# Silu in place of sigmoid and product, new engine orders, and a quarter of the threshold updates on GpSimd

## The reference

```
h = rmsnorm(x) * (1 + scale) + shift                 # adaLN from c
xr, gr, q, k, v, ga, qi, ki, wi = split(h @ w_in)    # 2760 columns
xr = causal conv of width 4;  y_r = rg_lru(xr) * silu(gr)
   gate_x, gate_a = sigmoid(...);  a = exp(-8 gate_a softplus(-a_param))
   h_t = a h_(t-1) + sqrt(1 - a^2) gate_x xr
score = sum over 8 heads of relu(qi . ki) * wi       # causal
idx = top 256 of each row of score                   # blocks of 128 rows
y_a = attention(q, k, v over idx only) * silu(ga)    # 8 heads of 64
x = x + gate * (concat(y_r, y_a) @ w_out);  out = rmsnorm(x)
```

## Time and profile before

| | |
|---|---|
| median of 3 runs (range) | 636.92 us (636.62 to 640.52) |
| the profiled execution | 639.16 us, of which the span is 637.4 us |
| PE busy | 540.3 us, 85% |
| VectorE busy | 444.1 us, 70% |
| ScalarE busy | 374.0 us, 59% |
| GpSimd busy | 247.5 us, 39% |

### The profile page before, as it was taken

One profiled execution on the slowest core, in us unless ns is written; L12 is line 12 of the kernel. 1 busy time (PEld: TensorE's weight loads), 2 busy tenths in 40 slices (PEclk: granted clock), 3 DMA queues, 4 the chain that ended last, 5 costly groups with the idle time before them and its releaser, 6 DMA issues. The chain is left out here.

```text
span 637.4 us, 8051 instructions
## 1 busy us (share of the span) xinstructions
PE 540.3 (85%) x2676; PEld 447.9 (70%) x2676; DVE 444.1 (70%) x996; ACT 374.0 (59%) x678; POOL 247.5 (39%) x207
## 2 busy tenths in 40 slices
PE   2369989979999996999999406478999999999994
PEld 2356868768777773888777305467888999988873
DVE  5985467767998978945778988856456665665532
ACT  7423236544698989865789334464556675656631
POOL 5050853252525466277656400750223030304322
PEclk9859989999999999899999855559999999999999
DMA  8966460341021121035450420030010001011011
GB/s 344 411 204 230 103 152 11 99 100 32 2 66 34 34 64 35 2 99 133 117 148 2 171 93 0 0 99 2 1 67 34 33 2 67 23 45 67 0 67 66
DMA packets 16457, 51.96 MB, mean 82 GB/s; under 512 B 4000, under 2 KB 5024, under 8 KB 15392
## 3 DMA queue, kind: packets, MB, share of 16 engines
q1 hardware_dynamic: 16416, 51.45, 25.6%
HBM read 37.81 MB, written 4.19 MB: 66 GB/s over the span
## 5 line engine op out<-in xcount | busy, mean ns | idle before, releaser
L1384 PE MATMUL pair<-h_hi,w_hi 128*128 128x512 f32 (+1 forms) x352 | 115.7, 411 | 7.7 <-DVE rnn_gr L1187 4.8
L1384 PE MATMUL pair<-h_lo,w_hi 128*128 128x512 f32 (+1 forms) x352 | 111.1, 397 | 0.0
L1384 PE MATMUL pair<-h_hi,w_lo 128*128 128x512 f32 (+1 forms) x352 | 110.1, 394 | 0.0
L1309 DVE TENSOR_TENSOR pt_lo<-pair,pt_hi 128x512 fp32r<-128x512 f32 (+3 forms) x96 | 50.5, 553 | 70.6 <-ACT pt_hi L968 70.2
L863 ACT ACTIVATE bias_sb<-score_sb,tinies 128x1024 bf16<-128x1024 f32 (+2 forms) x93 | 95.7, 1033 | 2.5 <-DVE tinies L1114 2.3
L1384 PEld LDWEIGHTS pair<-h_hi,w_hi 128*128 128x128 f32 (+1 forms) x352 | 65.7, 191 | 25.9 <-issue 13.8
L692 POOL TENSOR_SCALAR w_hi<-w_raw 128x1024 fp32r<-128x1024 f32 (+1 forms) x22 | 26.9, 1223 | 137.8 <-PE pair L1384 122.1
L1384 PEld LDWEIGHTS pair<-h_lo,w_hi 128*128 128x128 f32 (+1 forms) x352 | 66.8, 190 | 16.0 <-issue 1.1
L1384 PEld LDWEIGHTS pair<-h_hi,w_lo 128*128 128x128 f32 (+1 forms) x352 | 66.6, 189 | 15.7 <-issue 0.8
L1100 DVE TENSOR_SCALAR_CACHE_REDUCE bias_sb<-score_sb,tinies 128x640 bf16<-128x640 f32 (+2 forms) x93 | 72.5, 801 | 0.9
L782 POOL TENSOR_TENSOR x_res<-q_free,x_res 128x512 f32<-128x512 f32 x14 | 18.2, 1297 | 120.3 <-DVE q_free L1280 120.3
(11 more groups left out here) (199 smaller groups left out, 1258.9 us busy)
## 6 DMA issues: line engine op xcount, KB each, us to landing
w_raw<-in_w_tiles SPq DMA_DIRECT2D x21, 512.0 KB, 3.6
ada<-in_ada_w SPq DMA_DIRECT2D x8, 1024.0 KB, 18.1
x_sb<-in_x SPq DMA_DIRECT2D x8, 512.0 KB, 6.7
ada_g<-in_ada_w SPq DMA_DIRECT2D x8, 512.0 KB, 4.5
qs<-half_hi SPq DMA_DIRECT2D x16, 256.0 KB, 3.6
qs<-half_lo SPq DMA_DIRECT2D x16, 256.0 KB, 4.4
wo_raw<-in_w_out SPq DMA_DIRECT2D x8, 512.0 KB, 6.7
x_res<-in_x SPq DMA_DIRECT2D x8, 512.0 KB, 3.4
```

Source lines behind the costliest of these rows:

```text
L1309: nc.vector.tensor_tensor(pt_lo[:, 4 * b:4 * b + nc4, hh, :], psum[use % 2][:, 0:nc4 * P].rearrange("p (c q) -> p c q", q=P), f32(pt_hi[:, ...
L1384: ins = nc.tensor.matmul(psum[banks[half]][0:width, :], w[b][:, k, 0:width], hh[:, k, half * HALF:(half + 1) * HALF], start=(k == 0 and p ...
```

## The change

- `grm` is gone: ScalarE writes `Silu` of the gr tile straight into one of two buffers, `gr0` and `gr1`; TensorE's next-but-one tile waits for this (`silu_ok`).
- ga: one `Silu` in place of Copy, Tanh and GpSimd's three instructions.
- `update` in rounds 0 to 11 goes to GpSimd, each of the 36 as two instructions, the second an addition on one 16-bit half of the candidate. Rounds 12 to 30 stay on VectorE in the same form; at round 14 a memset is added to each of three. Its semaphores (`miss_a`, `cand_a`) are now one for each column.
- The halves on GpSimd (`split_slab`, q and qi halves, `pool_gx`, `yr`) are cut into pieces that are planned one by one, so that updates can stand between them.
- The evacuation of q waits no more for the stack DMAs nor for `gate_ok`, and that of kv and q waits for the last scan, not for the last `yr`. GpSimd's first piece of the q halves takes over the wait for the DMAs. The gate_b DMA waits for the last scan.
- The planner gets other costs, knows the activation tables (1.3 for a switch between silu, sigmoid, exp and sqrt), and so all orders of stages 2 and 3 are new.

```diff
-SPLIT_US = 3.9
-COUNT_A_US = (1.35, 1.25, 1.15)
-COUNT_US = (1.0, 0.87, 0.74)
-OWN_US = 0.55
-UPDATE_US = 0.44
+SPLIT_US = (1.1, 1.4, 1.4)
+COUNT_A_US = (1.38, 1.27, 1.16)
+COUNT_US = (0.98, 0.84, 0.71)
+OWN_US = 0.45
+UPDATE_US = 0.58
+UPDATE_LAG = 0.5
+POOL_ROUNDS = 12
+TABLE = {"silu": "silu", "sig": "sigmoid", "decay": "sigmoid", "root": "sqrt"}
...
-            add("DVE", ("update", it, c), UPDATE_US, 1, ("count_a", it, c), ("prep",))
+            add("POOL" if it < POOL_ROUNDS else "DVE", ("update", it, c), UPDATE_US, 1, (("count_a", it, c), UPDATE_LAG), ("prep",))
...
+        if event[0] in TABLE or event[0] == "evac" and TILES[event[1]][0] == "ga":
+            us += 1.3 * (table[0] != TABLE.get(event[0], "silu"))
+            table[0] = {"decay": "exp"}.get(event[0], TABLE.get(event[0], "silu"))
...
+        words = cand[:, :].bitcast(U16).rearrange("p (c h) -> p c h", h=2)
+        def update(engine, it, c):
+            engine.wait_ge(count_a, ACT_COLS * it + c + 1)
+            low = it >= 15
+            step = bit(it) if low else bit(it) >> 16
+            engine.tensor_scalar(miss[:, c:c + 1], cnt[:, c:c + 1], lim[:, c:c + 1], -float(step), ALU.is_gt, ALU.mult).then_inc(miss_a[c], 1)
+            engine.wait_ge(miss_a[c], it + 1)
+            if it == 14:
+                engine.memset(words[:, c, 0:1], 1 << 15)
+            half = words[:, c, int(not low):2 - int(low)]
+            engine.tensor_scalar(half, half, miss[:, c:c + 1], float(step // 2), ALU.add, ALU.add).then_inc(cand_a[c], 1)
...
-                nc.vector.tensor_scalar(cols(c, miss), cols(c, cnt), cols(c, lim), float(bit(it)), ALU.is_gt, ALU.mult).then_inc(miss_a, 1)
-                dve.wait_ge(miss_a, ACT_COLS * it + c + 1)
-                nc.vector.tensor_scalar(icand[:, c:c + 1], cols(c, miss), bit(it) >> 1, icand[:, c:c + 1],
-                                        ALU.bitwise_xor, ALU.bitwise_xor).then_inc(cand_a, 1)
...
                 if o[0] == "silu":
                     act.wait_ge(proj_done, J["gr", o[1]] + 1)
-                    if o[1]:
-                        act.wait_ge(grm_ok, o[1])
+                    if o[1] >= 2:
+                        act.wait_ge(rnn_done, 2 * (o[1] - 1))
-                    nc.scalar.activation(tg, pairs[J["gr", o[1]] % 2][:, :], ACT.Sigmoid).then_inc(silu_ok, 1)
+                    nc.scalar.activation(rnn[f"gr{o[1] % 2}"][:, :], pairs[J["gr", o[1]] % 2][:, :], ACT.Silu).then_inc(silu_ok, 1)
...
-                if kind in ("qi", "q"):
+                if kind == "qi":
                     act.wait_ge(stacked, 64 * QS.index(j))
...
-                    nc.scalar.activation(ga[:, n, :], src[:, :], ACT.Copy)
-                    ins = nc.scalar.activation(raw[:, :], src[:, :], ACT.Tanh, scale=0.5)
+                    ins = nc.scalar.activation(ga[:, n, :], src[:, :], ACT.Silu)
...
-                nc.vector.tensor_tensor(rnn["gr"][:, :], pairs[J["gr", ct] % 2][:, :], tg, ALU.mult).then_inc(grm_ok, 1)
...
                         elif before == "gr":
-                            pe.wait_ge(grm_ok, ct + 1)
+                            pe.wait_ge(silu_ok, ct + 1)
```

More of the change, by code:

```diff
@@ L24 @@
 I32 = mybir.dt.int32
+U16 = mybir.dt.uint16
 P = 128
@@ L135, in stages @@
             if k == 0:
-                need.append(("split", w) if w is not None else ("gacc", KC - 1))
+                need.append(("split", w, 2) if w is not None else ("gacc", KC - 1))
                 if j >= 2:
                     before = TILES[j - 2][:2]
-                    need.append({"xr": ("conv", before[1], 3), "gr": ("grm", before[1])}.get(before[0], ("evac", j - 2)))
+                    need.append({"xr": ("conv", before[1], 3), "gr": ("silu", before[1])}.get(before[0], ("evac", j - 2)))
             if j or k:
@@ L156, in stages @@
                 need.append(("idx", len(UNITS) - 1))
-            add("ACT", ("evac", j), {"gate": 1.05, "kv": 3.1, "q": 1.05}.get(kind, 2.1), 3, *need)
+            if kind == "ga":
+                need.append(("yr", CT - 1))
+            add("ACT", ("evac", j), {"gate": 1.05, "kv": 3.1, "q": 1.05, "ga": 1.05}.get(kind, 2.1), 3, *need)
             need = [("evac", j)]
@@ L164, in stages @@
                 need.append(("vlo",))
-            add("POOL", ("after", j), {"ga": 3.7, "qi": 2.7, "q": 3.9}.get(kind, 2.4), 3, *need)
+            if kind in ("qi", "q"):
+                add("POOL", ("half", j, 0), 1.3 if kind == "qi" else 1.1, 3, *need)
+                if kind == "q":
+                    add("POOL", ("half", j, 1), 1.3, 3, ("half", j, 0))
+                add("POOL", ("after", j), 1.35, 3, ("half", j, 0 if kind == "qi" else 1))
+            elif kind != "ga":
+                add("POOL", ("after", j), 2.45, 3, *need)
         if kind in ("kiwi", "kv"):
@@ L177, in stages @@
             c = n
-            prev = [("yr", c - 1)] if c else []
-            add("ACT", ("silu", c), 2.4, 2, done, ("grm", c - 1) if c else ("gacc", KC - 1))
-            add("DVE", ("grm", c), 1.3, 2, ("silu", c), *prev)
+            add("ACT", ("silu", c), 1.1, 2, done, ("yr", c - 2) if c >= 2 else ("gacc", KC - 1))
             for g in (0, 1):
@@ L199, in stages @@
             need.append(("kstep", SLAB_TILE[w - 2], KC - 1))
-        add("POOL", ("split", w), SPLIT_US, 5, *need)
+        for p in range(3):
+            add("POOL", ("split", w, p), SPLIT_US[p], 5, *(need if p == 0 else [(("split", w, p - 1), 0.0)]))
     add("PE", ("wi",), 0.9, 1, ("evac", 0), ("kstep", 1, KC - 1))
@@ L248, in stages @@
     slots = []
+    table = [""]
     todo = list(work)
@@ L700, in causal, with first_halves @@
                                         pattern=[[-1, P]], channel_multiplier=1).then_inc(masked, 1)
-            split_slab(0)
-            split_slab(1)
+            for p in range(3):
+                split_slab(0, p)
+            for p in range(3):
+                split_slab(1, p)
             stacks = [0]
+            def first_halves(j, part):
+                kind, n, _ = TILES[j]
+                if part == 0:
+                    pool.wait_ge(evac_done, EVAC[j] + 1)
+                    pool.wait_ge(stacked, 64 * stacks[0])
+                    if kind == "q" and n == 0:
+                        pool.wait_ge(v_ok, 1)
+                    stacks[0] += 1
+                if kind == "q" and part == 0:
+                    link(nc.gpsimd.tensor_scalar(half_hi[:, :], raw[:, :], 1.0, 0.0, ALU.mult, ALU.add))
+                else:
+                    nc.gpsimd.tensor_tensor(half_lo[:, 0:HALF], raw[:, 0:HALF], f32(half_hi[:, 0:HALF]), ALU.subtract)
             def after_evac(j):
@@ L733, in _ @@
                 if o[0] == "split" and o[1] >= 2:
-                    split_slab(o[1])
+                    split_slab(*o[1:])
+                if o[0] == "half":
+                    first_halves(*o[1:])
+                if o[0] == "update":
+                    update(pool, *o[1:])
                 if o[0] == "after":
```

108 lines of the change are left out of this document (46 added, 62 removed).

## The result

The changed kernel takes 630.64 us (median of 4 runs, 630.57 to 630.72) against 637.83 us of the kernel before in the same comparison: a ratio of 0.988, with an interval of 0.985 to 0.992. It is faster, by some 7 us instead of the 24.6 us forecast: 18.3 us above the 612.3 us forecast, and the forecast's range ended at 626. The profiled execution spans 628.8 us (before: 637.4).

What follows compares the result with a forecast made beforehand. Attention's start was taken as the bound, held back by VectorE's late search rounds. Starting it at 357.9 instead of 382.5 saves 24.6 us: 639.16 to 614.6 us profiled, 612.3 us as median; range 602 to 626 us.

Steps and rivals of the forecast that it cites:

- GpSimd's: Search rounds 0 to 11: 36 updates moved to GpSimd take 17 to 20 us, their delay costed at nothing.
- the sum: Counts' end 341.0 + 1.57 + `settle` 5.8 + 9.56 = attention's start 357.9, 24.6 us earlier; 612.3 us, chance 0.46.
- rival 4: Search: GpSimd updates late behind long pieces, slower than before; 672 us at 1.7 us late each; chance 0.04.
- TensorE, 350.8: Projections: 4.8 us stall for `grm` and 2.2 us of slow clock go, 7.0 us together, ending near 350.8.
- ScalarE, 341.0: Search counts' end: 351.6 less 20.3 of waits and 2.8 of copies, plus 3.8 of loads, gives 332.3; 341.0 taken.
- The middle: ScalarE's counts end between 337.3 (tile order) and 344.6 (only following TensorE); no row decided, so 341.0 was taken.
- 18 foreseen: VectorE in the search: 18 us less work, up to 29.6 us fewer waits, just enough to clear own rounds behind `settle`.
- rival 1: Attention's start: own columns' masks come early, TensorE becomes the bound, attention starts 31.3 us earlier; 605.6 us; chance 0.23.
- From attention's start to the end: Stretch from attention's first VectorE instruction to the span's end, taken as unchanged at 254.9 us.
- rival 3: Search: gain lost as ScalarE's 20 us and VectorE's waits return; within 1% of 636.9, say 634; chance 0.07.
- The signs that I had set for both: Projections after 353 us, VectorE's waits for ScalarE's counts over 15 us, or those counts waiting for GpSimd over 10 us.
- the signs of being right: Attention starting at 356 to 360 us, GpSimd waits under 5 us, no q DMA waits, three or four more table loads.

Runs made afterwards that it cites:

- without the hold: Changed kernel, same order, VectorE's recurrence operations replaced by copies of one source with an accumulated sum, recurrence left out: 619.9 us, 0.971.
- With no hold and the last Silu later: Changed kernel, recurrence replaced by one-source copies, last projection tile's Silu moved behind the last two counts in ScalarE's order: 614.9 us, 0.963.
- once less is held: Last Silu moved behind the last counts, added to the changed kernel with recurrence in 512-column halves (622.6 us) or replaced by one-source copies (614.9 us).
- halves: Recurrence operations split into 512 columns; here against measured durations, every update on VectorE and whole operations (620.1 us): 625.7 us, 0.979.
- the run with whole operations: Changed kernel planned anew with every update on VectorE and measured durations, recurrence operations of 1024 columns not split: 620.1 us, 0.971.

## Why the prediction was wrong

The step that failed is GpSimd's: "Undisturbed it takes 0.6 us. Behind one piece of 1.3 us it takes 1.9 us and is still in time; I cost it at nothing." I weighed GpSimd's own queue and not VectorE beside it, so the sum had no term for late updates. The first number was nearly right (0.30 and 0.31 us and a gap of 0.1, 0.7 in all). But the hold added 13 us to 36 updates, nearly all of it beside three recurrences, and there it once met both instructions of one update (213.72 and 214.44). ScalarE waited 17.0 us; without the hold the time is 10.8 us lower. The row was in hand: the earlier trace rows shows a piece of 3.14 us beside a scan, and I gave it to rival 4 with "there are three scans", as if the products beside them were free. The hold should have been a term of the sum. The rule that I named behind the rivals, of the Trainium skill, "GPSIMD Engine Reference", section Key points, says that GpSimd shares its SBUF interfaces with VectorE and contends with VectorE instructions that have two SBUF inputs or run in a two-port mode. The changed kernel's trace agrees for products (1.35 us), for scans (2.33 us) and for the fast tensor_scalar (0.70 us beside one of 0.68).

In the prediction's own terms, on the profiled run: the counts ended 25.0 us late (366.0 for 341.0), from there to attention's first VectorE instruction it took 11.0 us less (6.0 for 16.9), and from there to the end 1.9 more (256.8 for 254.9). That is the 16 us between 614.6 and the 630.57 us measured. The other 2.3 are the step from the profiled run to the median, which was 2.2 us before and is none now.

By its steps:
- *TensorE, 350.8.* The stall of 4.8 us went as said. "Nothing is added to TensorE" was wrong by consequence: three stalls, 11.6 us, for ScalarE's late results, and an end at 363.0. Without the hold it is 350.8.
- *ScalarE, 341.0.* The waits of 20.3 us did go, and the loads came: four more, 5.1 us, where the sum had three. A load ends at 191.37 and the activation behind it starts at 191.38, so no drain, as in the earlier trace rows. The q tiles' DMA wait is GpSimd's now. But new waits came: beside the 17.0 us for GpSimd, those for TensorE are 7.3 us at the Silus of ga and 6.9 us at q tiles, and they stay without the hold (7.7 and 7.5). Without the hold the counts end at 353.8. With no hold and the last Silu later the counts end at 350.8, 9.8 us after the 341.0. "The middle" between 337.3 and 344.6 was no bound at all: the new order ties the last rounds to TensorE's last tiles.
- *VectorE.* 14.0 us less busy time of 18 foreseen; all its waits for `yr` are gone, but those for ScalarE's counts are 23.1 us, as before, and 6.7 for ScalarE's `rnn_s` and 6.6 for a tile of TensorE are new, so VectorE waits 36.8 us where it waited 30.1. All the same no own round stood behind `settle`, and the own columns' masks were made before it, as in rival 1 and not in the sum. That made the way from the last count to VectorE's first instruction of attention 11.0 us shorter than in the sum, and hid that much of ScalarE's 25.0.
- *The tail.* The place of the last Silu, 3 us in the change and 4 to 5 once less is held (626.8 to 622.6, 619.9 to 614.9), was in no step. The load for exp was taken as hidden and isn't: 1.28 us at 375.53.
- *From attention's start to the end*: 254.9 us foreseen, 256.8 measured. ScalarE's `cmp` and the load delay the first exponential by 4.3 us against the kernel before, and from it on 2.4 us are gained; the cause of that gain wasn't tried.
- *Rivals.* What came is near rival 4's mechanism, late updates, though the updates themselves are held and not only a piece ahead of them, and with 10.8 us where it had 20 to 60. The outcome is rival 3's, which guessed 634 and had 0.07: ScalarE's 20 us did return, as waits for updates and tiles, and VectorE's too. The signs that I had set for both were right ones: projections after 353 us, VectorE waiting over 15 us for counts, and L905 (L863 before) waiting over 10 us for GpSimd. Of the signs of being right, no wait of TensorE for VectorE in the search stage, no ScalarE wait for q DMAs and four more table loads came too.

How much of the missing 18.3 us is what: 10.8 the hold, 3 to 5 the last Silu, and the 2.6 that are left between 614.9 and 612.3 are less than the spread of that run; errors of both signs stand behind them. The padded durations of the change are a separate loss of 5 us, seen where the updates are all on VectorE; the sum had no term for them. Left open: which part of the change without GpSimd's updates gives its 14 to 16 us, and why halves cost 5.6 us where GpSimd has no update (TensorE waits 4.6 us for ScalarE's copy of one raw tile there, against 2.4 in the run with whole operations; 1.9 us of its profile are a later start of the search).

## What to carry to other kernels

A small instruction that is moved to GpSimd to shorten a chain is only as quick as VectorE's instruction beside it lets it be: list what VectorE does in that stretch with two SBUF sources or in its fast mode, and count each as the latency of one GpSimd instruction. A planner for fixed orders needs that hold as a cost more than it needs padding; here it was worth 8 us in a few lines, which only made good what the hold had cost that plan. The gain over a plan with every update on VectorE, 4.4 us, came when half as many updates were moved and the long instructions were halved. And an evacuation that waits for the end of a stage doesn't belong ahead of work that could run without it.

## What the runs showed of the hardware

- The hold ends with the VectorE instruction and takes one GpSimd instruction at a time: 2.33 us beside scans of 1024 columns, 1.27 beside scans of 512. With copies of one source and an accumulator on VectorE, 72 instructions of 0.30 to 0.31 us show none.
- It seems to go the other way too. At 212.61 VectorE's tensor_scalar of 1024 columns (L1267), begun beside a piece of a weight split that GpSimd had under way from 212.36 to 213.63, took 1.56 us; in the kernel before, four of them (L1243) took 0.68 us each. That is one case in one trace, and no run tried it by itself.
- A VectorE instruction with one source in PSUM and one in SBUF doesn't hold a GpSimd instruction (two of 0.30 us beside one of 1.28). VectorE, and GpSimd beside it, in the changed kernel:
```profile
207.06 1.28 DVE L1210 SCALAR_TENSOR_TENSOR rnn_xc<-pair,sm,rnn_xc 128x1023 f32<-128x1023 f32 x1
```
```profile
207.36 0.30 POOL L611 TENSOR_SCALAR tinies<-tinies 128x1 uint16<-128x1 uint16 x1
207.76 0.30 POOL L606 TENSOR_SCALAR tinies<-tinies 128x1 f32<-128x1 f32 x1
```
- The same update is 0.21 and 0.22 us on VectorE, 0.30 and 0.31 on GpSimd; GpSimd's short operations of the earlier trace rows took 0.19, so they were no measure for these.
